# Convolution taps one product late, the bias ring behind them, and gates and adaLN rows moved

## The reference, cut to what matters

```python
h = h + 0.5 * ml[2] * swiglu(modulate(h, norm_g[i, 0], ml[0], ml[1]), ...)   # ml, mc = silu(c) @ ada_w + ada_b
def prep(t):
    qkv = silu(sum(xp[:, j:j + T] * w[j] for j in range(5)))     # centred convolution over time, then SiLU
    q, k = l2norm(q), l2norm(k)
    g = -exp(a_log) * softplus(ab[..., 0, :] + dt_bias)          # decay gates
    beta = sigmoid(ab[..., 1, :])
# chunked delta rule, forwards and backwards, on cumsum(g), beta, q, k, v
# neighbourhood attention: scores + bias table (na_rpb), masked, softmax, times v
```

## Time and profile before

| what | us |
| --- | --- |
| median of three runs | 3299.28 (3298.45 to 3299.69) |
| profiled execution | 3301.21 |
| its span, first to last instruction | 3299.4 |
| TensorE matmul busy | 3052.4 (93%) |
| VectorE busy | 1635.7 (50%) |
| ScalarE busy | 956.2 (29%) |
| GpSimd busy | 971.5 (29%) |

### The profile page before, as it was taken

The page is one execution under the profiler, slowest core; times in us unless marked ns, Lnnn a source line. Parts: engine busy times, 40 slices in busy tenths (PEclk is TensorE's granted clock), DMA queues, the critical chain, the costliest instruction groups (busy, mean ns, idle before and its releaser), DMA issues.

```text
span 3299.4 us, 45839 instructions
## 1 busy us (share of the span) xinstructions
PE 3052.4 (93%) x19072; PEld 2853.2 (86%) x19072; DVE 1635.7 (50%) x2480; ACT 956.2 (29%) x1611; POOL 971.5 (29%) x503
## 2 busy tenths in 40 slices
PE   6899999988978884799999999999999987899997
PEld 6899999988978883589999999999999876698996
DVE  5456666773545553537676668211222346531223
ACT  3211212433432222632212123211112336532222
POOL 0233333243221210123333333222222221344442
PEclk9999999999989996999999999999999999999999
DMA  5334454323200002123443432221221210132231
GB/s 201 114 108 137 127 138 127 107 93 108 88 16 1 1 1 77 49 77 128 136 133 122 146 129 85 68 64 58 64 65 55 78 45 1 39 96 91 89 96 65
DMA packets 119692, 282.63 MB, mean 86 GB/s; under 512 B 39870, under 2 KB 50878, under 8 KB 119230
## 3 DMA queue, kind: packets, MB, share of 16 engines
q1 hardware_dynamic: 116606, 272.24, 25.9%
q10 hardware_dynamic: 2880, 7.45, 0.6%
HBM read 268.08 MB, written 15.08 MB: 86 GB/s over the span
## 4 chain that ended last, share of the span: by engine, by line
PE 79%; DVE 9%; ACT 4%; issue 4%; POOL 2%; DMA 1%; SPq 0%; ACTq 0%; DVEq 0%; POOLq 0%
PE psum L1597 70%; DVE cacc L1255 2%; PE psum L1735 2%; PE psum L1727 2%; PE psum L1819 1%; PE psum L1812 1%; DVE o_acc L1410 1%; DVE prob_o L1543 1%; ACT prob_o L1136 1%; DVE sq L1223 1%; DVE probT_o L1552 0%; DVE prob_e L1543 0%; PE psum L1774 0%; DMA nqk<-spill 0%; PE psum L1741 0%
## 5 line engine op out<-in xcount | busy, mean ns | idle before, releaser
L800 POOL TENSOR_TENSOR wl<-raw,wh 128x1024 fp32r<-128x1024 f32 (+1 forms) x326 | 831.0, 2549 | 1744.1 <-ACT wh L886 1743.0
L1597 PE MATMUL psum<-uh,wh 128*128 128x256 f32 (+5 forms) x2704 | 666.5, 328 | 50.4 <-DVE sg L1223 19.3
L1597 PE MATMUL psum<-ul,wh 128*128 128x256 f32 (+5 forms) x2704 | 661.8, 326 | 0.0
L1597 PE MATMUL psum<-uh,wl 128*128 128x256 f32 (+5 forms) x2704 | 661.4, 326 | 0.0
L1597 PE MATMUL psum<-ah,wh 128*128 128x386 f32 (+4 forms) x2192 | 596.3, 344 | 5.9 <-POOL wl L800 4.8
L1597 PE MATMUL psum<-ah,wl 128*128 128x386 f32 (+4 forms) x2192 | 592.0, 342 | 0.0
L1597 PE MATMUL psum<-al,wh 128*128 128x386 f32 (+4 forms) x2192 | 589.9, 341 | 0.0
L1597 PEld LDWEIGHTS psum<-uh,wh 128*128 128x128 f32 (+1 forms) x2704 | 454.1, 190 | 75.9 <-issue 34.5
L1305 DVE SCALAR_TENSOR_TENSOR ada_product<-ada_w,cb 128x1024 f32<-128x1024 f32 x256 | 469.8, 1835 | 18.3 <-DMA ada_w<-in_ada_w 13.2
L1597 PEld LDWEIGHTS psum<-ul,wh 128*128 128x128 f32 (+1 forms) x2704 | 455.2, 191 | 19.2
L1597 PEld LDWEIGHTS psum<-uh,wl 128*128 128x128 f32 (+1 forms) x2704 | 453.3, 190 | 19.8
(11 more groups left out here) (208 smaller groups left out, 2544.1 us busy)
## 6 DMA issues: line engine op xcount, KB each, us to landing
raw<-in_w SPq DMA_DIRECT2D x264, 512.0 KB, 3.6
ada_w<-in_ada_w SPq DMA_DIRECT2D x128, 512.0 KB, 3.7
raw<-in_w SPq DMA_DIRECT2D x64, 448.0 KB, 3.6
spill<-cacc ACTq DMA_DIRECT2D x16, 384.0 KB, 2.3
scale_w<-in_scale_w SPq DMA_DIRECT2D x8, 512.0 KB, 14.4
ada_start<-in_ada_w SPq DMA_DIRECT2D x8, 512.0 KB, 14.6
ada_w<-bias_final SPq DMA_DIRECT2D x16, 256.0 KB, 3.1
h<-in_xT SPq DMA_DIRECT2D x8, 384.0 KB, 14.3
```

The costliest lines, as they stand in the source:

```text
L800: nc.gpsimd.tensor_tensor(wl[n % SPLIT_SLOTS][:, 0:k * w], raw[n % RAW_SLOTS][:, 0:k * w], wh[n % SPLIT_SLOTS][:, 0:k * w].bitcast(f32), A ...
L1597: ins = nc.tensor.matmul(pair[0:w, lo:hi], wt[n % SPLIT_SLOTS][:, k * w:(k + 1) * w], xt[:, k, cols], start=first, stop=last)
```

## The change

- `ada_plan` leaves out the three fused items: the eight chunks of term 2 go to the 13 items behind norm 0.
- norm 0 takes a PSUM pair but does not advance the rotation, so up 1 takes its pair, gate 2 that of gate 0, and so on; every later rotating item stands one pair further back than before.
- ScalarE takes a one-column root of eps ahead of the start loop.
- VectorE does the taps of convolution c at the next projection, behind its scaling; ScalarE takes the SiLU of c at the projection after that, ahead of its wait for the scaled product.
- The bias ring starts at projection 12 (ab) instead of 1; its last wait and the three loads come at k = 14.
- ScalarE's gates stand behind nv 0, VectorE's behind nv 1, and the item cum between nv 2 and nv 3.

```diff
-    at = [i for i, x in enumerate(items) if x[0] in ("gate", "up", "down") and x[1:3] == (0, 0)]
+    at = [i for i, x in enumerate(items) if x[0] in ("gate", "up", "down") and x[1:3] == (0, 0)][FUSED:]
...
-        s += [x] + norms[i:i + 1]
-    s += [("cum",)]
+        s += [x] + norms[i:i + 1] + ([("cum",)] if x == ("proj", 0, "nv", 2) else [])
...
-                turn += 1
+                turn += x != ("norm", 0)
...
                 if x[0] == "proj" and x[1] == 0:
-                    k = proj_order.index(x) - 1
+                    k = proj_order.index(x) - 12
...
-                    if k == 16:
+                    if k == 14:
...
                 elif x[0] == "proj" and x[1] == 0:
-                    n = proj_order.index(x) - 1
+                    n = proj_order.index(x) - 12
...
-            unsilued = [None]
-
-            def conv_silu():
-
-                if unsilued[0] is not None:
-                    c = unsilued[0]
+            def conv_silu(c):
+
+                if 0 <= c < 12:
                     act.wait_ge(conv_tap, 4 * c + 4)
                     nc.scalar.activation(dqkv[:, c // 4, c % 4, :], cacc[c % 2][:, :], ACT.Silu).then_inc(convolved, 1)
-                    unsilued[0] = None
 
             def finish_product(x):
 
+                if x[0] == "proj" and x[1] == 0:
+                    conv_silu(proj_order.index(x) - 2)
                 act.wait_ge(scaled, scaled_no[x] + 1)
...
                     ins.then_inc(conv_centre, 1)
-                    conv_silu()
-                    unsilued[0] = c
...
+            nc.scalar.activation(std[:, 0:1], eps[:, :], ACT.Sqrt)
             for k in range(KD):
                 act.wait_ge(x_loaded[k], 16)
...
+                    if x == ("proj", 0, "nv", 0):
+                        gates()
...
-                elif x in conv_no:
-                    c = conv_no[x]
-                    dve.wait_ge(conv_centre, c + 1)
...
+                if x[0] == "proj" and x[1] == 0:
+                    conv_taps(proj_order.index(x) - 1)
+
+            def conv_taps(c):
+
+                if not 0 <= c < 12:
+                    return
+                dve.wait_ge(conv_centre, c + 1)
+                for n, j in enumerate((0, 1, 3, 4)):
+                    sh = j - 2
+                    if n:
+                        dve.wait_ge(conv_tap, 4 * c + n)
+                    for (lo, hi), t, _ in pieces(proj_order[c]):
...
+                    if x == ("proj", 0, "nv", 1):
+                        gates()
```

More of the change, by code:

```diff
@@ L1010, in finish_product, with gates @@
                     nc.scalar.activation(to, t, ACT.Identity, bias=b).then_inc(odd_read, 1)
+            def gates():
+                act.wait_ge(ab_read, 1)
+                nc.scalar.activation(sp_a[:, :, :], ab[:, :, 0:8], ACT.Abs).then_inc(gate_chain, 1)
+                act.wait_ge(gate_chain, 1)
+                nc.scalar.activation(sp_e[:, :, :], sp_a[:, :, :], ACT.Exp, scale=-1.0).then_inc(gate_chain, 1)
+                act.wait_ge(gate_chain, 2)
+                nc.scalar.activation(sp_a[:, :, :], sp_e[:, :, :], ACT.Ln, bias=1.0).then_inc(gate_chain, 1)
+                nc.scalar.activation(ea[:, :], rows[:, 0:8], ACT.Exp).then_inc(gate_chain, 1)
+                nc.scalar.activation(beta[:, :, :], ab[:, :, 8:16], ACT.Sigmoid).then_inc(gate_chain, 1)
             act.dma_start(c_cols[:, :, :], a["c_cols"]).then_inc(c_cols_loaded, 16)
@@ L1071, in _ @@
                 elif x[0] == "cum":
[L1073 to L1080, removed]
                     act.wait_ge(product_done, i + 1)
@@ new lines, in conv_taps @@
+            def conv_taps(c):
[7 more added lines that the diff above has]
+                    for (lo, hi), t, _ in pieces(proj_order[c]):
+                        first, last = lo - min(sh, 0), hi - max(sh, 0)
+                        acc = cacc[c % 2][:, first:last]
+                        ins = nc.vector.scalar_tensor_tensor(out=acc, in0=t[:, first + sh - lo:last + sh - lo],
+                                                             scalar=conv_w[:, c, j:j + 1], in1=acc, op0=ALU.mult, op1=ALU.add)
+                    ins.then_inc(conv_tap, 1)
@@ new lines, in gates @@
+            def gates():
+                dve.wait_ge(gate_chain, 5)
+                nc.vector.scalar_tensor_tensor(out=decay[:, :, :], in0=ab[:, :, 0:8], scalar=0.0, in1=sp_a[:, :, :],
+                                               op0=ALU.max, op1=ALU.add).then_inc(gate_chain, 1)
+                dve.wait_ge(gate_chain, 6)
+                nc.vector.scalar_tensor_tensor(out=decay[:, :, :], in0=decay[:, :, :], scalar=-1.0,
+                                               in1=ea[:, :].unsqueeze(1).to_broadcast([P, STEPS, 8]),
+                                               op0=ALU.mult, op1=ALU.mult).then_inc(gates_ready, 1)
```

8 lines of the change are left out of this document (removed).

## The result

| | before | after |
| --- | --- | --- |
| median, us | 3299.49 (3298.45 to 3304.49, 4 runs) | 3248.84 (3246.52 to 3249.25, 4 runs) |
| profiled execution, us | 3301.21 | 3249.25 |
| its span, us | 3299.4 | 3247.5 |
| granted clock, mean | 0.974 | 0.979 |

The ratio is 0.9841 (95% interval 0.9826 to 0.9857): 50.7 us faster, where the forecast was 57. Both profiles were cut at the same places, the first matmul of TensorE in each stage. "Forecast" is what the prediction's steps give for the same stretch.

A forecast was written before the change was run, and what follows sets the result against it. TensorE was taken as the bound, gains coming from its idle time: -19.8 - 25.7 - 1.9 + 1.5 - 12.5 - 0.5 + 1.9 = -57.0 from 3301.2, giving 3244.2, median 3242 us; range 3234 to 3258.

The forecast's parts named there:

- First root: Start, behind norm 0: TensorE resumes 18.2 us earlier, plus 1.6 of clock; -19.8 us, bounds -16.5 to -20.8.
- Convolutions: Convolved projections: late taps drop VectorE's 2.35 wait, so TensorE sets the pace; -25.7 us, and -1.9 for the clock behind.
- Rival B: Convolution loop stays above TensorE's pace, 9.3 a product instead of 8.5; +10, 3252 us; chance 0.11.
- Ring: Key stage: moved bias adds on GpSimd delay VectorE's multiply 0.2 to 0.25, six times; +1.5 us, bounds 0 and 6.2.
- Rival E: Bias ring closes a loop between SP and GpSimd, +9 a product over twelve products; +109, 3351 us; chance 0.03.
- Gates: Last projection to DeltaNet: earlier gates and cum close the 13.5 hole, 1.0 late; -12.5 us, and -0.5 for the clock.
- rival D: Gates' change fails its aim: the last projection's weights come another product late; +8, 3250 us; chance 0.04.
- Banks: Layer 1 value transposes, in the shifted PSUM rotation, wait for rotary 9; +1.9 us, 0 at best.
- Rival C: TensorE restarts early at the first root but halts at ("up", 2), only VectorE's 12.2 counts; 3249 us; chance 0.09.

The follow-up runs named there:

- the last two experiments: Two edits of the kernel before: only the taps one projection later (SiLU two later), 3270.8 us; only the bias ring moved to start at projection 12, 3293.61 us.

## Why the prediction held, and where it did not

**First root: right, 1.5 too small.** TensorE resumed 2.44 us behind the norm's first matmul, where the sum had 2.48 (72.07 to 74.55), and the feed-forward behind it took 540.76 instead of 543.37, -2.6 where I took -1.6 for the clock: with a pause of 0.99 us the grant stayed at 1.00, the better of the two outcomes between which I had set my value. The last 0.4 is the earlier norm, which is chance. Of the change's parts, taking back the chunks costs 12.9 and taking back the bank 7.8; the preload is worth nothing, because the table load does not wait for the norm (last section).

**Convolutions: right.** -28.1 against -27.6. The step that VectorE's loop falls to TensorE's pace held with room: 7.8 us of work and 0.75 of waiting. The forecast of the taps without the ring (7.4) was too high, 6.83, and the one with it (7.50, 8.5 for the loop) too high as well, 7.32. The prediction had both loops tie with TensorE's pace, 8.5 with the ring's adds and 8.4 without them; the last two experiments and that with the ring in its old place show that with late taps the ring's move has no part in the gain. The half microsecond by which the result is better is the pace: 8.49 was taken for a product at full clock from a stretch that began with 5.8 us at the lower one, and 540.76 us for 64 products are 8.45. Rival B is excluded by the same rows.

**Ring: the mechanism right, the term undersized, +2.4 for +1.5.** Six multiplies are longer, as forecast, but by 0.40 (1.36 against 0.96) where I took 0.25: 6 x 0.40 = 2.4. The estimate took 1.03 for an add, as beside the taps, and so had the multiply meet the end of the first. Beside the reciprocal an add takes 0.73, the first is over when the multiply comes, and it meets the second with 0.53 to 0.56 still to run. The seventh, with no ring item beside it, is at 0.96. The Trainium skill, "SBUF — State Buffer", section "Who interferes with whom", calls it an exclusive lock: the trace agrees in that the multiply pays 0.38 to 0.42 us, most of what is left of the one add in flight, in each of six cases, and the 12.4 of a queued second add did not come. Rival E, the closed loop of SP and GpSimd, is excluded: of the 9 us a product that it names, the longest wait for a split in the stage is 1.10, and the stage lost 2.4 us in all.

**Gates: the step that failed.** The sum had 13.5 less 1.0: 0.8 for cum on TensorE and 0.2 for weights that come late. I added the gates' 6.46 us to the copy's place in ScalarE's queue, and read that place from the earlier trace rows, where the copy stands at item nv 1. But the change also puts an item, cum, into the list, and "two items on" is counted in items. From nv 1 the second next item is now cum, which has no weights; the copy moved to nv 2. It is the mechanism of rival D ("the last projection's weights come another product late", chance 0.04) at a smaller price, 4.75 us in place of its 8. In the sum's terms: it had 0.2 for weights that come late, and with the clock behind them they cost 4.75. With the copy put in front of the gates the gain is 12.9, beside the 12.7 of the sum without the late weights. So the gates' own part was right, and the look-ahead was the error. No run changes the count alone; that it is the count and not the gates in front rests on the rows, where the gates end 2.8 us before the copy starts, and on the kernel's text.

**Banks: the place right, the term undersized.** I had the wait, +1.9 (measured 3.30 against 1.38), but no clock. TensorE idles 2.2 us there instead of 0.3, and behind it transposes, scores and the next transposes run at the lower grant, 0.79 over the 32 us against 0.94 before. Taken back by itself the border is worth 3.7. The 5.3 between the two traces is more than that, and the other traces settle why: with the old banks at this place the stretch takes 27.9 to 28.5 us in five experiments, with the shifted ones 31.3 to 32.4 in six, and the 26.89 of the kernel before is 1.0 below them all. So 3 to 4 us belong to the change, and the rest is chance.

**The rest.** From the DeltaNet on to rotary 9 the difference is -2.3 where -0.5 was forecast. Up to norm 2 it is -0.4, about the forecast. The other 1.9 come between norm 4 of the list and rotary 9, where TensorE waits less for a weight load (3.44 us against 4.77) and keeps its clock. That wait is anywhere from 3.44 to 4.89 in the thirteen traces, with nothing near it edited, so it is not put down to the change: it is luck that hid part of what the gates and the banks cost.

The time came in the range because the range was wide enough for three terms that all erred to the same side, and small gains beside them, the largest of which, 1.9 us between norm 4 and rotary 9, nobody forecast. The forecast minus the result: 57.0 less 51.9 are 5.1 us; further, I took the profiled execution to be 1.9 above the median, and after it was 0.4, which makes the other 1.5. Rival C stood at 3249, which is the time that came, but its mechanism did not: no wait stands at ("up", 2). An equal time is no evidence for a rival.

## What to carry to other kernels

Where an engine executes something "for the items up to two on", inserting an item moves work of every engine that counts so: redo the count for the two items ahead of the insertion before adding up delays. An edit that makes a pacing engine fast enough makes others superfluous that work on the same idle time, so price each edit with the others in place; here the late taps alone bring the convolutions' whole gain and the ring's move only its cost. And with a pause of 1 to 3 us of TensorE put the clock behind it into the range and not into the sum: 0 or some 1.5 us here, for the same pause at the same place.

## What the runs showed of the hardware

- A pause of 3.02 us ahead of the last projection was followed by a product at a granted clock of 0.83, 10.09 us instead of 8.54; without the pause (weights ahead) the clock stayed at 1.00. But the same pause of 3.03 in the trace with the chunks ahead was followed by a product of 8.54 us at 1.00, the only one of seven such traces. In the same way the pause of 2.84 in the last product ahead of norm 0 cost nothing in the changed kernel (18 matmuls in 3.07 us) and 1.3 with the taps undone (4.33), from the same code. Pauses of 0.99 and 1.07 us at the first root cost nothing; those of 2.97, 7.05 and 7.40 there were each followed by 3 to 4 us in which two matmuls take 0.85 us and not 0.51.
- The table load of an activation does not wait for what the activation waits for: without the preload it ran from 70.02 to 71.30, with the root right behind at 71.31, while the matmuls that the root reads ended near 71.2. The Trainium skill, "ScalarE: Activation LUTs", section "What ACT_TABLE_LOAD costs", gives 2.66 us for a switch by load and drain; in the gates of the changed kernel the loads at 853.54 and 855.09 are 1.55 us apart with an activation of 0.24 between them, so the load's 1.28 is seen here and the drain is not.
- A VectorE product of two SBUF operands beside a split of GpSimd, 90.77, took 3.42 us where it takes 1.22 alone; the l2 multiply beside an add took 1.36 instead of 0.96. GpSimd pays too: the two adds of a ring item take 2.07 beside the taps and 1.40 to 1.43 beside the reciprocal. The reciprocal, of one operand, takes 4.95 beside a split alone and beside a split and two adds, and the scaling out of PSUM 0.96 with and without a split beside it.
- Where TensorE never pauses, the time repeats: the first feed-forward of layer 1 takes 560.30 or 560.31 us in all thirteen traces. From the DeltaNet to norm 2, with its many short pauses, it is 554.14 to 558.26 in six traces whose code there is the same. So an effect of 2 to 4 us is read from its own stretch and not from the median of two runs.
